# First scan: the second visit's outputs go through ScalarE and GpSimd instead of VectorE

## What is computed

```python
def mlstm_outputs(q, k, v, log_i, log_f, pre):
    ...
    num = einsum('bhnts,bhnsv->bhntv', s, vc) + a[..., None] * einsum('bhntk,bhnvk->bhntv', qc, c_prev)
    den = sum(s, axis=-1) + a * einsum('bhntk,bhnk->bhnt', qc, n_prev)
    h = num / maximum(abs(den), exp(-m))[..., None]
...
y_lat = out_fn(*lat_f, pre_lf) + flip(out_fn(*lb, pre_lb), axis=2)     # forward scan + backward scan
y_ml  = head_rms_norm(h_ml, g_ml) * sigmoid(p[..., OFF_ML_O:OFF_ML_G]) # per-head norm, then output gate
```

## Time and profile before

| | |
|---|---|
| median of 3 runs | 1369.33 us (1368.87 to 1370.21) |
| the profiled execution's own time | 1369.33 us |
| its span, first to last instruction | 1367.6 us |
| busy: TensorE / VectorE / ScalarE / GpSimd | 1281.7 / 948.0 / 773.7 / 118.7 us |
| mean granted clock of TensorE | 0.979 of full speed |

### The profile page before, as it was taken

The page is one execution under the profiler, slowest core; times in us unless marked ns, Lnnn a source line. Parts: engine busy times, 40 slices in busy tenths (PEclk is TensorE's granted clock), DMA queues, the critical chain, the costliest instruction groups (busy, mean ns, idle before and its releaser), DMA issues.

```text
span 1367.6 us, 19538 instructions
## 1 busy us (share of the span) xinstructions
PE 1281.7 (94%) x7427; PEld 1119.6 (82%) x7427; DVE 948.0 (69%) x1114; ACT 773.7 (57%) x918; POOL 118.7 (9%) x127
## 2 busy tenths in 40 slices
PE   6899999898999999989999399999999999999994
PEld 4888799888987999877888388888888888888883
DVE  5757420357755672476544878888888888888887
ACT  6643320474312643574334357777777777777785
POOL 1100000010000000013000020111111111111034
PEclk9999999999999999999999699999999999999997
DMA  9851151233444312304122869999999999999995
GB/s 377 276 106 34 62 167 34 63 108 97 173 193 179 124 68 94 139 1 170 78 77 111 350 245 372 380 406 403 384 406 390 398 401 396 391 397 399 395 318 211
DMA packets 78686, 320.45 MB, mean 234 GB/s; under 512 B 5544, under 2 KB 32200, under 8 KB 48856
## 3 DMA queue, kind: packets, MB, share of 16 engines
q1 hardware_dynamic: 71360, 291.18, 54.3%
q0 software_dynamic: 7264, 28.40, 8.1%
HBM read 292.20 MB, written 35.75 MB: 240 GB/s over the span
## 4 chain that ended last, share of the span: by engine, by line
PE 76%; DVE 12%; ACT 4%; issue 4%; DMA 3%; SPq 0%; POOLq 0%; DVEq 0%; ACTq 0%
PE psum L2540 36%; PE psum L2194 6%; PE psum L2476 6%; PE psum L2252 5%; PE psum L2254 5%; PE psum L2253 5%; PE psum L2280 1%; DMA ada_raw<-w_ada_units 1%; DVE ml_c L1586 1%; PE psum L2095 1%; PE psum L2563 1%; ACT g_ps L1121 1%; PE psum L2557 1%; PE psum L2497 1%; DVE left L1927 1%
## 5 line engine op out<-in xcount | busy, mean ns | idle before, releaser
L1957 DVE TENSOR_TENSOR e_lo<-e_raw,e_hi 128x2048 fp32r<-128x2048 f32 x192 | 432.8, 2287 | 43.2 <-ACT e_hi L1271 43.2
L1271 ACT ACTIVATE e_hi<-e_raw 128x2048 fp32r<-128x2048 f32 x192 | 365.9, 1917 | 83.0 <-PE psum L2540 81.9
L2540 PE MATMUL psum<-e_hi,xt_hi 128*128 128x512 f32 x496 | 153.3, 390 | 0.1
L2540 PE MATMUL psum<-e_lo,xt_hi 128*128 128x512 f32 x496 | 152.9, 389 | 0.0
L2540 PE MATMUL psum<-e_hi,xt_lo 128*128 128x512 f32 x496 | 152.9, 389 | 0.0
L2252 PE MATMUL psum<-w_hi,h_hi 128*128 128x256 f32 x512 | 147.6, 288 | 0.5 <-issue 0.5
L2253 PE MATMUL psum<-w_hi,h_lo 128*128 128x256 f32 x512 | 146.2, 286 | 0.0
L2254 PE MATMUL psum<-w_lo,h_hi 128*128 128x256 f32 x512 | 146.2, 285 | 0.0
L2540 PEld LDWEIGHTS psum<-e_hi,xt_lo 128*128 128x128 f32 x496 | 93.1, 188 | 19.6
L2540 PEld LDWEIGHTS psum<-e_lo,xt_hi 128*128 128x128 f32 x496 | 93.1, 188 | 19.5
L2540 PEld LDWEIGHTS psum<-e_hi,xt_hi 128*128 128x128 f32 x496 | 92.8, 188 | 19.8 <-DVE xt_lo L1961 0.5
(11 more groups left out here) (414 smaller groups left out, 2310.7 us busy)
## 6 DMA issues: line engine op xcount, KB each, us to landing
e_raw<-w_e_units SPq DMA_DIRECT2D x192, 1024.0 KB, 7.7
ada_x<-w_ada_units SPq DMA_DIRECT2D x16, 1024.0 KB, 4.9
raw<-w_in_units SPq DMA_DIRECT2D x14, 1024.0 KB, 6.1
bc<-rows_dram SPq DMA_DIRECT2D x18, 512.0 KB, 3.8
ada_raw<-w_ada_units SPq DMA_DIRECT2D x8, 1024.0 KB, 21.8
xs<-x SPq DMA_DIRECT2D x4, 1024.0 KB, 11.0
acc_dram<-zero_r SPq DMA_DIRECT2D x1, 4096.0 KB, 18.9
wo_raw<-w_out SPq DMA_DIRECT2D x4, 1024.0 KB, 6.1
```

What stands on the lines that cost most here:

```text
L1271: act.activation(e_hi[u % EH][:], e_raw[u][:], ACT.Copy).then_inc(e_hi_ok, 1)
L1957: dve.tensor_tensor(e_lo[u][:], e_raw[u][:], e_hi[u % EH][:], ALU.subtract).then_inc(e_lo_ok, 1)
L2540: m = pe.matmul(o[:, BANK * b:BANK * (b + 1)], x[:, k, :], w[:, D * j + BANK * b:D * j + BANK * (b + 1)], start=a, stop=z)
```

## The change

In second visits ScalarE now writes `num_ps` times 1/den into a spare row, `h_new` (512 columns in 128 partitions), and GpSimd adds that row to `h_ml`. VectorE does neither. ScalarE waits before it writes `h_new` until the add before is done; the counter for it, `h_added`, is a semaphore that was used earlier in the launch and stands at 8. The square `h_sq` waits for all eight adds.

```diff
+        h_new = at("h_new", AT_OUT + 44 * KB, [P, ML_W])
...
+        h_added, H_BASE = conv_free, 8
...
+            def h_add(l):
+                c = scan_chunk(l)[1] - TC
+                pool.wait_ge(h_done, l + 1)
+                pool.tensor_tensor(h_ml[:, c, :], h_ml[:, c, :], h_new[:], ALU.add).then_inc(h_added, 1)
+
             for l in range(2 * TL):
                 d = l % 2
                 pool.wait_ge(e_done, l + 1)
                 pool.affine_select(out=ml_w[d][:], in_=ml_w[d][:], compare_op=ALU.is_ge, fill=0.0, base=0,
                                    pattern=[[0, NH], [1 - 2 * d, P]], channel_multiplier=2 * d - 1).then_inc(w_ready, 1)
+                if l >= TL + 2:
+                    h_add(l - 2)
+            h_add(2 * TL - 2)
+            h_add(2 * TL - 1)
...
             def ml_back(t, l, d, c):
-                if l is None or not first_visit(d, c):
+                if l is None:
                     return
                 act.wait_ge(num_mm, l + 1)
                 act.wait_ge(den_seq, 3 * l + 3)
+                to = h_ml[:, c - TC, :]
+                if not first_visit(d, c):
+                    to = h_new
+                    act.wait_ge(h_added, H_BASE + l - TL)
                 for h in range(NH):
-                    i = act.activation(h_ml[:, c - TC, HD * h:HD * (h + 1)], num_ps[:, h // 2, h % 2, 0:HD], ACT.Copy,
+                    i = act.activation(to[:, HD * h:HD * (h + 1)], num_ps[:, h // 2, h % 2, 0:HD], ACT.Copy,
                                        scale=den[:, d, h:h + 1])
                 i.then_inc(h_done, 1)
...
-            act.wait_ge(h_done, 2 * TL)
+            act.wait_ge(h_added, H_BASE + TL)
             act.activation(h_sq[:], h_ml[:], ACT.Square).then_inc(ml_norm, 1)
...
-                if first_visit(d, c):
-                    return
-                dve.wait_ge(den_seq, 3 * l + 3)
-                at_least(dve, h_done, l)
-                for h in range(NH):
-                    o = h_ml[:, c - TC, HD * h:HD * (h + 1)]
-                    i = dve.scalar_tensor_tensor(o, num_ps[:, h // 2, h % 2, 0:HD], den[:, d, h:h + 1], o, ALU.mult, ALU.add)
-                i.then_inc(h_done, 1)
```

## The result

The changed kernel took 1376.42 us (median of 11 runs, 1372.86 to 1380.72), the kernel before, run beside it, 1370.76 us (11 runs, 1368.87 to 1376.51). The ratio is 1.0032 with a 95% interval of 1.0020 to 1.0044: slower, by 4.4 us (2.7 to 6.0). The two medians lie 5.7 us apart, more than that ratio says; executions of either kernel differ among themselves by about 8 us, and with 11 of each both figures are loose. The direction is the one forecast. The level is not: 1372.8 was forecast, with a range to 1374.0. The profiled execution of the changed kernel took 1372.86 us, the shortest of its 11. That it lies within 0.1 us of the forecast is partly luck: the profiled execution of the kernel before was a low one too.

A forecast was written before the change was run, and what follows sets the result against it. TensorE was taken as the bound, held in the scan by a ring with VectorE. Later o_hi 2.55, minus vanished o_lo wait 1.06, plus clock fall 2.0, made 3.5; 1369.33 + 3.5 = 1372.8 us, range 1370.4 to 1374.0.

The forecast's parts named there:

- The ring: Scan step: L2280, outputs, VectorE's den and state update, next L2280 hold TensorE; second visits go from 4.627 to 4.59 us.
- the wait for `o_lo`: Behind the scan: TensorE's 1.06 us wait vanishes, because matmuls on o_hi at the low clock take 3.7 us.
- the loss: At the scan's end: late o_hi and slower clock cost 3.5 us together, with 3.0 and 3.9 at the ends.
- The low level: TensorE behind the scan: after 4.3 us idle, 1.2 GHz lasts 3.75 to 5.9 us, costing 2.0 us.
- The add: GpSimd in each second-visit step: 1.04 us, fits with the 0.63 us mask in a step of 4.59 us.
- The forecast's own range: Whole kernel: 1372.3 to 1373.5 us, with about 0.7 us scatter of the runs on top.
- straight on: TensorE behind the scan: goes on with o_hi at 339.26, then waits 1.06 us for o_lo.
- The argument on the clock: TensorE at the scan's end: idle stretches of 3.15 and 19.52 us preceded a low clock, so 4.3 us lowers it too.
- The clock holds: Rival: TensorE's clock doesn't fall behind the scan; 1369.33 + 1.6 = 1371.0 us; 20%.
- VectorE's time counts: Rival: scan steps shrink by up to 1.12 us each as VectorE drops h_ml; 1364.1 us; 5%.
- The delay is hidden: Rival: TensorE has slack behind o_lo that absorbs the delay; time stays at 1369.3 us; 5%.
- GpSimd gets in VectorE's way: Rival: each add stretches VectorE's work by 0.37 us, seven steps cost 2.6 us more; 1375.4 us; 4%.

The follow-up runs named there:

- before_o_hi_late: Kernel before, with ScalarE made to wait for all of h_ml before it writes o_hi: 1375.24 us (9 runs), ratio 1.0026.
- after_filled: Changed kernel with 18 small identity multiplications on TensorE behind the scan, while it waits for o_hi: 1373.95 us (11 runs), ratio 1.0019.
- before_again: Kernel before, unedited, run against itself with a second trace: 1370.56 us (12 runs), ratio 0.9998.
- before_third: Kernel before, unedited, run against itself with a third trace: 1371.72 us (12 runs), ratio 0.9998.
- o_hi_early: Changed kernel with ScalarE writing o_hi ahead of the last two chunks' outputs: 1370.53 us, ratio 0.9989 to the kernel before; repeated, 1370.76 us, 0.9995.
- o_lo_first: Kernel before, with VectorE writing o_lo ahead of the last chunk's h_ml: 1369.34 us (12 runs), ratio 0.9982; repeated, 1369.05 us, 0.9978.

## Why the prediction was right in its difference and wrong in its level

**What held.** The ring doesn't pass through VectorE's `h_ml`: taking it away gave 4.58 instead of 4.627 us a step, as forecast (4.59). `o_hi` started at 339.79 (forecast 339.83), TensorE at 341.81 (341.81) after 4.31 us idle (4.3). The clock fell, the wait for `o_lo` vanished, and the loss came to 3.4 us from the scan's start to `o_lo` (3.5, with ends 3.0 and 3.9). The low level lasted 5.1 us behind the restart (3.75 to 5.9) and cost 1.9 us (2.0). Two experiments separate the parts: `before_o_hi_late` shows that the place of `o_hi` alone makes the loss, `after_filled` that 1.9 us of it hang on the fall of the clock.

**What failed: the step from the difference to a time.** The prediction says "The profiled execution took exactly the median, 1369.33 us, so the sum is 1369.33 + 3.5", and of the range "with the scatter of the runs shown, about 0.7 us, on top". Both lean on three runs. The 102 runs of the kernel before that were made beside the others, those three among them, have a median of 1371.48 us and reach from 1368.58 to 1376.6 (the 24 runs of `before_again` and `before_third` added, the median is the same and the lowest 1368.27). The three were low ones, and so was the profiled execution: only 7 of the 102 took less. Their spread of 1.34 us said little about the scatter, which is 8 us. The stretch to A alone took 253.8, 255.1 or 257.3 us in three traces of the same program, and falls of the clock in the other stages come and go. The 3.6 us between 1376.42 and 1372.8 split so: 1371.48 - 1369.33 = 2.15 for the base; 0.5 because the difference of the pooled medians is 1375.47 (29 runs) - 1371.48 = 4.0 rather than 3.5; and 1376.42 - 1375.47 = 0.95 because those 11 runs of the changed kernel lay above its pooled median.

**A term that was missing.** end - D is 571.6 us in each of the six traces without the change and 571.9 to 572.0 in each of the seven with it. It is VectorE's last instruction, which follows the one before by 1.38 us before (1357.67 to 1359.05) and by 1.76 us after. The prediction has no term for it:

```profile
1357.67 1.28 DVE L2078 SCALAR_TENSOR_TENSOR y_exp<-y_exp,rstd,psum 128x1024 f32<-128x1024 f32 x1
1359.05 1.22 DVE L2080 TENSOR_TENSOR y_exp<-y_exp,x_rows 128x1024 f32<-128x1024 f32 x1
```

```profile
1360.78 1.28 DVE L2085 SCALAR_TENSOR_TENSOR y_exp<-y_exp,rstd,psum 128x1024 f32<-128x1024 f32 x1
1362.54 1.23 DVE L2087 TENSOR_TENSOR y_exp<-y_exp,x_rows 128x1024 f32<-128x1024 f32 x1 [0.48 <-DVE y_exp L2085]
```

With it the traces give 3.4 + 0.4 = 3.8 us, beside the 4.0 of the pooled medians. What makes those 0.4 us stays open. The instructions there are the same; elsewhere VectorE has 32 fewer, ScalarE 32 and GpSimd 8 more. One more thing goes with it, which the pages show, before and after:

```profile
q14 instruction: 18, 0.15, 0.0%
```

```profile
q14 instruction: 19, 0.16, 0.0%
```

These are transfers of instructions. The six traces without the change have 18, the seven with it 19. Whether the one more has to do with the 0.4 us no run shows, and no experiment was made on it.

**What was mis-sized or overlooked, without effect on the time.** The add takes 1.27 us, not 1.04: the row it was sized by reads one tensor twice. The trace of before has the right row two lines further on, L788, with two different inputs, at a median of 1.27 us. It fits all the same. The forecast's own range ends at 1373.5, but its sum with 3.9 us ends at 1373.2. TensorE does not go "straight on" with `o_hi`: the earlier trace rows has it idle 1.47 us for `ml_c`, as the prediction itself uses later.

The argument on the clock was thinner than it reads. The trace of before has, besides the launch's first 7 us, a third idle stretch of over 3 us: 3.86 us before 21.76, behind which the window 20 to 30 us shows a granted clock of 1.00, though eight matmuls of L2106 took 1.91 us at 37.29, as at the low level. And it has two falls with TensorE busy, which the prediction did not look at: the granted clock is 0.86 over 180 to 205 us, with TensorE busy 24.45 us of 25, and 0.89 over 450 to 465, busy all 15. So the clock also falls without a long idle stretch. That this one goes with the idle time is shown by `after_filled` and not by the rows of before. The prediction also did not see that the change could take 1.06 us off the scan's end, since with `h_ml` gone nothing stands ahead of `o_lo` on VectorE. With `o_hi` in time the change is worth 1.4 us there, 92.5 to 91.1; as written, VectorE waits 2.82 us for `o_hi` before it can start `o_lo`, and nothing of that gain is left.

**The rivals.** *The clock holds*: it fell in all three traces of the changed kernel and in `before_o_hi_late`; in the filled kernel it held, and B - A grew by 1.5 us (forecast 1.6). *VectorE's time counts*: refuted by the step of 4.58. *The delay is hidden*: refuted by the table, where C - B and D - C don't shrink. *GpSimd gets in VectorE's way*: not in the steps, which took 4.58 us. It did meet `o_lo` in `o_hi_early`, where GpSimd was the one slowed.

## What to carry to other kernels

When an engine is given more to do in a loop, look first at what stands right behind the loop in that engine's code and who waits for it: here one instruction of 1.93 us, which used to lie in idle time, cost more than all the moved work could gain. Ask of an unloaded engine not how much less it does, but what it can now start earlier; here that part was had by two moved lines, without the rest. And take a level and its scatter from more than three runs, or forecast the difference and say that the level is only known to the scatter of single executions.

## What the hardware showed that was not expected

- The same program, executed again, spends different amounts of time at TensorE's low clock: near 453 us 3.3 or 6.9 us in the kernel before, none or 3.3 us in `o_lo_first`, each 3.4 us of it costing 1.5 us. TensorE was busy 13.9 to 15.0 us of those 15.
- GpSimd's addition of two rows of 128x512 takes 1.27 us alone and 2.28 us beside a VectorE instruction of 128x2048 with two inputs in SBUF, whose own time (2.29 us) stayed what it was; both traces of `o_hi_early` have the 2.28. In the one shown it ended 1.14 us behind the VectorE instruction (341.88 + 2.28 - 343.02), little less than its own 1.27, as if it had stood nearly still until then. That is an estimate from the rows; none shows the waiting itself.
- The last two VectorE instructions of the launch, 1000 us behind the change, came 0.4 us further apart in all seven traces that have it; the cause is open.
